# Side loads on a second queue, 64x64 taps in pairs, splits inside the norms, and routing over both token halves

## The chip, the cores and the metric

One Trainium2 chip, and one of its cores. The metric is the time of one execution of the kernel on the device, in microseconds; a kernel's time is the median over runs. A NeuronCore has separate engines with their own instruction streams: TensorE (PE), VectorE (DVE), ScalarE (ACT), GpSimd (POOL) and SyncE (SP). DMA transfers are issued from an engine's queue.

## The reference

Two blocks over 256 tokens of 1024 channels, in fp32. The part that matters here, with its parameters shortened:

```python
def conv_module(h, w_in, b_in, w_dw, b_dw, g_n, b_n, w_out, b_out):
    a, g = jnp.split(h @ w_in + b_in, 2, axis=-1)
    u = a * jax.nn.sigmoid(g)
    u = lax.conv_general_dilated(u, w_dw[:, None, :], window_strides=(1,), padding=[(CONV_K - 1, 0)],
        dimension_numbers=("NWC", "WIO", "NWC"), feature_group_count=u.shape[-1]) + b_dw   # 31 taps
    u = jax.nn.silu(layer_norm(u, g_n, b_n))
    return u @ w_out + b_out

def moe_swiglu(h, router_w, router_b, w13, w2):
    logits = (h @ router_w).astype(jnp.float32) + router_b.astype(jnp.float32)
    top_val, top_idx = lax.top_k(logits, TOP_K_EXPERTS)          # 2 of 8 experts
    top_w = jax.nn.softmax(top_val, axis=-1)
    gates = jnp.sum(jax.nn.one_hot(top_idx, N_EXPERTS) * top_w[..., None], axis=-2)
    for e in range(N_EXPERTS):
        y = y + gates[..., e:e + 1] * swiglu(h, w13[e], w2[e])
    return y

def first_block(x, c, ...):                                       # 256 tokens, 1024 channels, fp32
    c_act = jax.nn.silu(c)
    for l in range(2):
        sh1, sc1, g1, sh2, sc2, g2 = jnp.split(c_act @ ada_w[l] + ada_b[l], 6, axis=-1)
        h = x * (1.0 + sc1[:, None, :]) + sh1[:, None, :]
        out = conv_module(h, ...) if l == 0 else moba_attention(...) @ w_o[0]
        x = layer_norm(ALPHA * x + (1.0 + g1[:, None, :]) * out, ln_g[l, 0], ln_b[l, 0])
        h = x * (1.0 + sc2[:, None, :]) + sh2[:, None, :]
        f = swiglu(h, ffn_w13[0], ffn_w2[0]) if l == 0 else moe_swiglu(h, ...)
        x = layer_norm(ALPHA * x + (1.0 + g2[:, None, :]) * f, ln_g[l, 1], ln_b[l, 1])
    return x
# second_block: layer norm, band attention beside an rwkv7 scan, gates, layer norm,
# hier_moe (4 groups of 8 experts: the best group, 2 in it), layer norm, a gated projection, layer norm
```

## The kernel before

All weights are streamed. A list `units` holds them in the order of use, as pieces of 1 MB (128 partitions x 2048 fp32, two DMAs of 512 KB). SP issues their loads into the six slots of `ring_raw` as these come free. For fp32 accuracy, a product is three matmuls of rounded parts: ACT makes the high part of a unit (`split_hi`, into one of three slots of `ring_hi`, L442), DVE the low part (`split_lo`, `ring_lo`, L460), and PE's `columns` runs hi x hi, lo x hi and hi x lo (L2186 to L2188) per 128x128 block: 48 matmuls of 256 columns a unit. The activations have hi and lo parts too (`Hh`/`Hl`, `Gh`/`Gl`). The adaptive units ("ada": 24 for layer 0, 8 for kv, 24 for layer 1) aren't split: `adaptive` (L2223) multiplies an fp32 unit by the vector c on four column quarters of PE, and for each pair `turn_row` (L2236) turns ACT's copy of the row (`row_out`, L2507) into columns; DVE adds the bias (`biased`, L2867) to give `mods`.

The order is written out by hand, one list per engine, with semaphores between them. It goes:

1. start: ada 0 to 5 on PE, then transposes (L2243) of 40 short parameter rows (in `tA`) and of x (`tB`), ada 6 and 7, then ACT writes `Hh` (L2530) and DVE `Hl`. SP issues the ada loads, the row loads, x and the first router's loads (L1912) and then further units.
2. conv_in (8 units), then the depthwise convolution of 31 taps over 8 channel blocks. PE has three blocks and part of a fourth (`SHARED`, 17 taps): a tap is a matmul of a 128x128 diagonal with the shifted `uT` (L2315), all taps of a block summed in one bank. POOL writes the diagonals (L1820). DVE has the other blocks (`conv_dve`, L1806) and the rest of the shared one (L2904). `conv_order` puts five taps of PE behind each of the 16 ada units 8 to 23.
3. the conv norm: `ln_stats` on PE (mean L2264, variance L2270), `ln` on DVE (centre L2812, reciprocal L2818, scale L2823) with ACT squaring (L2476) between, `Gh`/`Gl`; then conv_out (4 units), ln0 of the same form, the FFN (11 pairs "ffn a"/"ffn b" and their down units), ln1, kv and q.
4. attention a1, interleaved with ada units of layer 1 by `between(i)`; the output product wo (4 units); ln2; and MoE m1: DVE ranks the logits (L1495 to L1507) for each half of the 128 tokens in turn, PE counts the chosen (L1214 to L1218), rows are gathered by matmul (L1237), and 56 groups of 6 units follow.
5. ln3, the second block with band attention and rwkv (L584, L610 are 64x64 matmuls of its chunked scan), MoE m2 (routing as in m1, 16 groups of 6 units), a gated projection and the output.

`ln` takes a function that it runs on DVE between the centre and the reciprocal, where DVE waits for PE's variance; m1's norm uses it, the conv norm and ln0 don't. `keep_busy` runs matmuls whose results nobody reads (L2252).

## Time and profile before

| | |
|---|---|
| median of 3 runs | 2388.09 us (2386.42 to 2390.18) |
| the profiled execution | 2391.7 us, its span 2389.9 us |
| busy share of the span | PE 95%, DVE 72%, ACT 58%, POOL 4% |
| mean granted clock of PE | 0.972 |
| chain that ended last | PE 88%, DVE 5%, ACT 3%, issue 2%, DMA 1%, SP's queue 1% |
| HBM | 257 GB/s over the span, 614 MB read |

The profile is of one execution, and its times are from the start of the span. "[2.32 <-ACT scr L2507]" means that the engine was idle for 2.32 us before the instruction, and what ended this. Short runs of one instruction are joined to a row with their count. A matmul of fp32 leaves two records, one of rounded operands one.

### The profile page before, as it was taken

Reading aid. Unit: us, or ns where it says so; the run is one execution under the profiler, and the core shown is the slowest. Engines: PE = TensorE matmul, PEld = TensorE weight load, DVE = VectorE, ACT = ScalarE, POOL = GpSimd, SP = SyncE. Lnnn points to the kernel's source line nnn. Section 1 sums busy time; section 2 is a strip of 40 time slices with the busy share of each in tenths; the row PEclk is TensorE's granted clock in tenths of the full one; section 3 lists DMA queues with packets and bytes.
Section 4 is the critical chain, followed back from the end, with each engine's and each line's share of the span. In section 5 each row is a group of like instructions: output and inputs, shape, how many; then the busy total and the mean of one; then the engine's idle time right before and its main releaser. Section 6 shows DMA issues by size and latency. Waiting matters only on the chain.

```text
span 2389.9 us, 36267 instructions
## 1 busy us (share of the span) xinstructions
PE 2274.6 (95%) x14695; PEld 1961.4 (82%) x14695; DVE 1730.1 (72%) x1723; ACT 1376.6 (58%) x1291; POOL 91.5 (4%) x140
## 2 busy tenths in 40 slices
PE   6997999998899999999999999999998897999998
PEld 4876999996788888888888888888997796888887
DVE  2885344636678888888888888884676467999954
ACT  3234333536567777777777777773465334777743
POOL 5600000001000000000000000000000000000000
PEclk9998999999899999999999999999999898999999
DMA  9665665359179999999999999995741231999930
GB/s 297 214 217 192 231 228 180 105 176 326 63 255 343 394 376 367 374 368 372 371 372 370 371 370 373 369 370 73 198 128 37 83 123 61 348 368 370 376 127 19
DMA packets 339267, 618.78 MB, mean 259 GB/s; under 512 B 24615, under 2 KB 165168, under 8 KB 339100
## 3 DMA queue, kind: packets, MB, share of 16 engines
q1 hardware_dynamic: 339100, 616.43, 73.9%
q8 instruction: 120, 1.97, 0.3%
q14 instruction: 47, 0.39, 0.0%
HBM read 614.26 MB, written 1.05 MB: 257 GB/s over the span
## 4 chain that ended last, share of the span: by engine, by line
PE 88%; DVE 5%; ACT 3%; issue 2%; DMA 1%; SPq 1%; DVEq 0%; ACTq 0%
PE bank L1264 11%; PE bank L1265 11%; PE bank L1266 11%; PE bank L2186 6%; PE bank L2187 6%; PE bank L2188 6%; PE bank L1296 6%; PE bank L1298 6%; PE bank L1294 6%; PE bank L2270 2%; PE bank L1237 1%; PE bank L2315 1%; PE bank L1274 1%; PE bank L1328 1%; PE bank L584 1%
## 5 line engine op out<-in xcount | busy, mean ns | idle before, releaser
L1379 DVE TENSOR_TENSOR ring_lo<-ring_raw,ring_hi 128x2048 fp32r<-128x2048 f32 x432 | 988.4, 2291 | 140.4 <-ACT ring_hi L1372 139.8
L1372 ACT ACTIVATE ring_hi<-ring_raw 128x2048 fp32r<-128x2048 f32 x432 | 828.0, 1920 | 297.3 <-PE bank L1266 177.2
L1264 PE MATMUL bank<-ring_hi,xg_hi 128*128 128x512 f32 x1152 | 458.2, 398 | 2.3 <-DVE xg_lo L1575 2.1
L1265 PE MATMUL bank<-ring_hi,xg_lo 128*128 128x512 f32 x1152 | 451.0, 391 | 0.0
L1266 PE MATMUL bank<-ring_lo,xg_hi 128*128 128x512 f32 x1152 | 450.9, 391 | 0.0
L2186 PE MATMUL bank<-Hh,ring_hi 128*128 128x256 f32 x1048 | 305.5, 291 | 31.0 <-DVE ring_lo L460 9.7
L460 DVE TENSOR_TENSOR ring_lo<-ring_raw,ring_hi 128x2048 fp32r<-128x2048 f32 (+1 forms) x96 | 217.9, 2283 | 138.7 <-ACT ring_hi L442 129.5
L2188 PE MATMUL bank<-Hh,ring_lo 128*128 128x256 f32 x1048 | 301.5, 288 | 0.0
L2187 PE MATMUL bank<-Hl,ring_hi 128*128 128x256 f32 x1016 | 292.8, 288 | 0.0
L1264 PEld LDWEIGHTS bank<-ring_hi,xg_hi 128*128 128x128 f32 x1152 | 217.5, 189 | 48.2 <-ACT xg_hi L1434 2.8
L1266 PEld LDWEIGHTS bank<-ring_lo,xg_hi 128*128 128x128 f32 x1152 | 217.1, 188 | 47.2
L1265 PEld LDWEIGHTS bank<-ring_hi,xg_lo 128*128 128x128 f32 x1152 | 217.6, 189 | 43.4
L2186 PEld LDWEIGHTS bank<-Hh,ring_hi 128*128 128x128 f32 x1048 | 206.3, 197 | 36.5 <-issue 24.7
L442 ACT ACTIVATE ring_hi<-ring_raw 128x2048 fp32r<-128x2048 f32 (+1 forms) x96 | 181.2, 1897 | 88.9 <-PE bank L2188 68.2
L1294 PE MATMUL bank<-ring_hi,mh 128*128 128x512 f32 x576 | 228.4, 396 | 0.0
L1296 PE MATMUL bank<-ring_hi,mh 128*128 128x512 f32 x576 | 228.2, 396 | 0.0
L1298 PE MATMUL bank<-ring_lo,mh 128*128 128x512 f32 x576 | 228.1, 396 | 0.0
L2188 PEld LDWEIGHTS bank<-Hh,ring_lo 128*128 128x128 f32 x1048 | 206.6, 197 | 0.0
L2187 PEld LDWEIGHTS bank<-Hl,ring_hi 128*128 128x128 f32 x1016 | 200.7, 198 | 0.1
L1298 PEld LDWEIGHTS bank<-ring_lo,mh 128*128 128x128 f32 x576 | 108.4, 188 | 26.2
L1296 PEld LDWEIGHTS bank<-ring_hi,mh 128*128 128x128 f32 x576 | 108.5, 188 | 25.8
L1294 PEld LDWEIGHTS bank<-ring_hi,mh 128*128 128x128 f32 x576 | 108.4, 188 | 25.7
(490 smaller groups left out, 2829.7 us busy)
## 6 DMA issues: line engine op xcount, KB each, us to landing
ring_raw<-in_moe_w SPq DMA_DIRECT2D x672, 512.0 KB, 5.3
ring_raw<-in_ada_w SPq DMA_DIRECT2D x96, 512.0 KB, 6.2
ring_raw<-in_ffn_w SPq DMA_DIRECT2D x66, 512.0 KB, 5.4
ring_raw<-in_exp_gate SPq DMA_DIRECT2D x64, 512.0 KB, 4.6
ring_raw<-in_exp_up SPq DMA_DIRECT2D x64, 512.0 KB, 4.7
ring_raw<-in_exp_down SPq DMA_DIRECT2D x64, 512.0 KB, 4.7
ring_raw<-in_w_in SPq DMA_DIRECT2D x42, 512.0 KB, 5.0
ring_raw<-in_conv_in_w SPq DMA_DIRECT2D x16, 512.0 KB, 8.1
```

Source lines behind the costliest of these rows:

```text
L460: nc.vector.tensor_tensor(ring_lo[:, i % SPLIT, 0:kt * c], ring_raw[:, n % RAW, 0:kt * c], ring_hi[:, i % SPLIT, 0:kt * c].bitcast(F32), A ...
L1264: mm(o, xg_hi[:, g, kk, :], wh(k), start=(kk == 0), stop=False)
L1265: mm(o, xg_lo[:, g, kk, :], wh(k), start=False, stop=False)
L1266: last = mm(o, xg_hi[:, g, kk, :], wl(k), start=False, stop=(kk == KT - 1))
L1294: mm(o, mh_hi[:, 2 * h + k, :], wh[:, k, ns], start=begin, stop=False, skip_group_check=True)
L1296: mm(o, mh_lo[:, 2 * h + k, :], wh[:, k, ns], start=False, stop=False, skip_group_check=True)
L1298: last = mm(o, mh_hi[:, 2 * h + k, :], wl[:, k, ns], start=False, stop=end, skip_group_check=True)
L1372: nc.scalar.activation(ring_hi[:, at % SPLIT, :], ring_raw[:, n % RAW, :], ACT.Copy)\
L1379: nc.vector.tensor_tensor(ring_lo[:, at % SPLIT, :], ring_raw[:, n % RAW, :], ring_hi[:, at % SPLIT, :].bitcast(F32), ALU.subtract).then_i ...
L2186: mm(o, wh[:, k, cs], Xh[:, k, :], start=(k == 0), stop=False)
L2187: mm(o, wh[:, k, cs], Xl[:, k, :], start=False, stop=False)
L2188: last = mm(o, wl[:, k, cs], Xh[:, k, :], start=False, stop=(k == kt - 1))
```

## The change

- **Loads.** x (now two DMAs) and the parameter rows are issued by ACT, right behind its first activation; SP keeps the units. The router's two loads stand ahead of conv_out 0's. PE runs ada 6 ahead of x's transposes.
- **Taps.** PE has four blocks whole or in part (the shared one, block 4, with 8 taps): 101 taps instead of 79. A diagonal is 128x64 (two 64x64 diagonals, one above the other). Taps go in pairs: of tap i the rows 0 to 63 and 64 to 127 are added to their own halves of the bank `dw`, of tap i+1 to the other halves of a bank `dx`. When a block is through, ACT copies `dx` to `scr`, and one matmul with a permutation (`perm`) adds it to `dw` with the halves swapped. Behind each ada unit stand three pairs, or four.
- **Norms.** In the conv norm and ln0, a `split_lo` of the next weight unit moves into the gap of `ln`, others move behind the halves that PE needs; `biased("turn kv")` comes behind the first pair of `affine_lo`. conv_out 0 waits for each k block by itself; `keep_busy` before it has 12 matmuls, not 20.
- **ffn and wo.** `biased("turn 1 1")` moves from the end of j = 3 to j = 4, behind `split_lo`. The splits of wo 0 move into the attention's last steps, `fold_in("m1")` behind them, and wo 0 waits for each head pair by itself.
- **Routing.** In m1 and m2 DVE's ranking takes both token halves in one instruction each; the counts take three matmuls, not five.

```diff
@@ -33,7 +33,7 @@
...
-PE_BLOCKS = 3
+PE_BLOCKS = 4
...
-            mm(b[:, 0:m.E], before[:, :], sel[:, 0, :], start=True, stop=True)
-            mm(b[:, m.E:2 * m.E], ones[:, :], sel[:, 0, :], start=True, stop=False)
-            mm(b[:, m.E:2 * m.E], before[:, :], sel[:, 1, :], start=False, stop=True)
-            for a in range(TT):
-                last = mm(b[:, 2 * m.E:3 * m.E], ones[:, :], sel[:, a, :], start=(a == 0), stop=(a == 1))
+            first_half = sel[:, 0:1, :].to_broadcast([P, TT, m.E])
+            mm(b[:, 0:2 * m.E], before[:, :], sel, start=True, stop=False, skip_group_check=True)
+            mm(b[:, m.E:3 * m.E], ones[:, :], first_half, start=False, stop=False, skip_group_check=True)
+            last = mm(b[:, 2 * m.E:3 * m.E], ones[:, :], sel[:, 1, :], start=False, stop=True, skip_group_check=True)
...
-            for a in range(TT):
-                rank(L[:, a, 0:E], 8, R, sel[:, a, 0:E])
-                ts(sel[:, a, 0:E], sel[:, a, 0:E], 1.5, None, ALU.is_lt).then_inc(dve.tick(), 1)
+            selE, shE = sel[:, :, 0:E], sh[:, :, 0:E]
+            by_group = lambda t: t[:, :, 0:E].rearrange("p a (g e) -> p (a g) e", e=8)
+            rank(by_group(L), 8, TT * R, by_group(sel))
...
+            T.mark(f"{nm} sel", *dve.last)
+            ts(shE, selE, -NEG, NEG, ALU.mult, ALU.add).then_inc(dve.tick(), 1)
+            dve.eng.wait_ge(*dve.own())
+            tt(shE, shE, L[:, :, 0:E], ALU.add).then_inc(dve.tick(), 1)
+            dve.eng.wait_ge(*dve.own())
+            nc.vector.tensor_reduce(rmax[:, :, 1:2], shE, AX, ALU.max, negate=True).then_inc(dve.tick(), 1)
...
-        SHARED, ON_PE = KT - PE_BLOCKS, 17
+        SHARED, ON_PE = KT - PE_BLOCKS, 8
         pe_taps = [(k, i) for k in pe_blocks for i in range(ON_PE if k == SHARED else TAPS)]
         last_tap = lambda k: ON_PE - 1 if k == SHARED else TAPS - 1
-        tiles = lambda t, n: [t[:, P * i:P * i + P] for i in range(n)]
-        diag = dict(zip(pe_taps, tiles(flat(GhF), 16) + tiles(flat(GlF), 16) + tiles(flat(convd), 16)
-                        + tiles(prF, 9) + tiles(prTF, 9) + tiles(flat(tB), 16) + tiles(flat(tD), 16)))
-        conv_order, taps_left = [], list(pe_taps)
+        tiles = lambda t, n: [t[:, 64 * i:64 * i + 64] for i in range(n)]
+        diag = dict(zip(pe_taps, tiles(flat(GhF), 32) + tiles(flat(GlF), 32) + tiles(flat(convd), 32) + tiles(prF, 18)))
+        tap_pairs = [(k, i) for k, i in pe_taps if i % 2 == 0]
+        swapped = scr[:, 1, :]
+        conv_order, taps_left, to_swap = [], list(tap_pairs), []
         for j in range(8, 24):
             conv_order.append(("ada", j))
-            for _ in range(5):
+            conv_order += [("swap", to_swap.pop(0)) for _ in range(len(to_swap))]
+            for _ in range(3 if j % 4 else 4):
                 if taps_left:
-                    conv_order.append(("tap", taps_left.pop(0)))
-        conv_order += [("tap", t) for t in taps_left]
+                    k, i = taps_left.pop(0)
+                    conv_order.append(("tap", (k, i)))
+                    if i + 2 > last_tap(k):
+                        to_swap.append(k)
+        assert not taps_left
+        conv_order += [("swap", k) for k in to_swap]
...
-            for n, (k, i) in enumerate(pe_taps):
-                if n == 66:
-                    pool.eng.wait_ge(*T.at("mm x 3"))
-                if n == 82:
-                    pool.eng.wait_ge(*T.at("Hl conv"))
-                nc.gpsimd.tensor_scalar(diag[k, i], ident[:, :], col("conv_dw_w", k, i), None, ALU.mult)\
+            for k, i in pe_taps:
+                nc.gpsimd.tensor_scalar(diag[k, i], m_one[:, :], col("conv_dw_w", k, i), None, ALU.mult)\
                     .then_inc(pool.tick(f"diag {k} {i}"), 1)
...
-                if what == "tap" and which[1] == last_tap(which[0]):
+                if what == "tap" and which[1] + 2 > last_tap(which[0]):
                     k = which[0]
                     act.eng.wait_ge(*T.at(f"mm dw {k}"))
+                    if k != SHARED:
+                        act.eng.wait_ge(*T.at(f"mm swap {k - 1}"))
+                    nc.scalar.activation(swapped, ps(f"dx {k}")[:, 0:S], ACT.Copy).then_inc(act.tick(f"ev dx {k}"), 1)
+                if what == "swap":
+                    k = which
+                    act.eng.wait_ge(*T.at(f"mm swap {k}"))
                     nc.scalar.activation(tA[:, k, :], ps(f"dw {k}")[:, 0:S], ACT.Identity, bias=col("conv_dw_b", k))\
...
@@ -1858,6 +1868,7 @@
...
+                if key == ("conv_out", 0):
+                    small_load("m1 router landed", rw[:, :, 0:8], A["router_w"][0].rearrange("(k p) n -> p k n", p=P))
+                    small_load("m1 router landed", rbias[:, 0:8], A["router_b"].to_broadcast([P, 8]))
...
+                            pe.eng.wait_ge(*T.at(f"hi {fresh} {k // 2 if fresh == 'convo' else k}"))
+                            pe.eng.wait_ge(*T.at(f"lo {fresh} {k if fresh == 'a1 o' else k // 2}"))
...
+            adaptive(0, 6, first)
...
-            for j in range(6, 8):
-                adaptive(0, j, first)
+            adaptive(0, 7, first)
...
+                if what == "swap":
+                    k = which
+                    pe.eng.wait_ge(*T.at(f"ev dx {k}"))
+                    mm(dw[:, 0:S], perm[:, :], swapped, start=False, stop=True, skip_group_check=True)\
+                        .then_inc(pe.tick(f"mm swap {k}"), 1)
+                    continue
...
-                    dw = take(pe, f"dw {k}", "C")
+                    dw, dx = take(pe, f"dw {k}", "C"), take(pe, f"dx {k}", "C")
                     pe.eng.wait_ge(*T.at(f"ev conv a {k // 2}"))
-                pe.eng.wait_ge(*T.at(f"diag {k} {i}"))
-                last = mm(dw[:, 0:S], diag[k, i], uT[:, k, i:i + S], start=(i == 0), stop=(i == last_tap(k)))
-                if i == last_tap(k):
-                    last.then_inc(pe.tick(f"mm dw {k}"), 1)
+                for tap in (i, i + 1):
+                    if tap > last_tap(k):
+                        continue
+                    pe.eng.wait_ge(*T.at(f"diag {k} {tap}"))
+                    for r in range(2):
+                        rows = slice(64 * r, 64 * r + 64)
+                        at = rows if tap == i else slice(64 - 64 * r, 128 - 64 * r)
+                        last = mm((dw if tap == i else dx)[at, 0:S], diag[k, tap][rows, :], uT[rows, k, tap:tap + S],
+                                  start=(i == 0), stop=(tap + 2 > last_tap(k)), skip_group_check=True)
+                        if tap + 1 > last_tap(k):
+                            last.then_inc(pe.tick(f"mm dw {k}"), 1)
...
-            keep_busy(20, "C")
-            pe.eng.wait_ge(*T.at("Gh conv"))
-            pe.eng.wait_ge(*T.at("Gl conv"))
+            keep_busy(12, "C")
             for j in range(4):
-                columns(("conv_out", j), f"out0 {j}", Gh, Gl)
+                columns(("conv_out", j), f"out0 {j}", Gh, Gl, None if j else "convo")
...
-            pe.eng.wait_ge(*T.at("Hh wo"))
-            pe.eng.wait_ge(*T.at("Hl wo"))
             for j in range(4):
-                columns(("wo", j), f"wo {j}", Hh, Hl)
+                columns(("wo", j), f"wo {j}", Hh, Hl, None if j else "a1 o")
...
+            x_in = tB[:, :, :].rearrange("p (a k) t -> p a (k t)", a=TT)
+            for a in range(TT):
+                small_load("x landed", x_in[:, a, :], A["x"][0, a * P:(a + 1) * P, :])
+            rows = tA[:, 0:4, :].rearrange("p k t -> p (k t)")
+            act.eng.wait_ge(*T.at("rows cleared"))
...
+            for name, src, n, width in sources:
+                r = ROW[name]
+                small_load("rows landed", rows[r:r + n, 0:width], src)
...
+                if i == 16:
+                    split_hi(act, at_unit[("wo", 0)])
...
                 for j in range(4):
+                    if j == 1 and behind_first:
+                        behind_first()
...
-            conv_dve(dve, range(2, KT - PE_BLOCKS), done)
-            dve.eng.wait_ge(*T.at(f"ev dw {SHARED}"))
-            for i in range(ON_PE, TAPS):
-                stt(tA[:, SHARED, :], uT[:, SHARED, i:i + S], col("conv_dw_w", SHARED, i), tA[:, SHARED, :],
-                    ALU.mult, ALU.add).then_inc(dve.tick(f"z conv {SHARED}"), 1)
-                dve.eng.wait_ge(*dve.own())
+            for i in range(ON_PE):
+                done[SHARED, i] = T.at(f"ev dw {SHARED}")
+            conv_dve(dve, range(2, KT - PE_BLOCKS + 1), done)
+            def in_conv_norm():
+                split_lo(dve, at_unit[("conv_out", 0)])
+                biased("turn rest", [(0, v) for v in range(2, 6)])
+            ln("conv", None, in_conv_norm)
+            halves_lo("convo", Gl, tD, Gh)
             split_lo(dve, at_unit[("conv_out", 1)])
-            biased("turn rest", [(0, v) for v in range(2, 6)])
-            ln("conv")
-            halves_lo("convo", Gl, tD, Gh)
             T.mark("Gl conv", *dve.last)
             dve.eng.wait_ge(*T.at("mods 0 2"))
             tt(gb[:, :], cols[:, :, ROW["conv_out_b"]], mods[:, VEC(0, 2), :], ALU.mult).then_inc(dve.tick("gb"), 1)
             fold_in("ffnin")
             residual("ln0", "out0", "conv_out")
+            ln("ln0", None, lambda: split_lo(dve, at_unit[("ffn a", 0)]))
+            affine_lo("ffnin", tD, Hl, Hh, lambda: biased("turn kv", [(2, 0), (2, 1)]))
+            T.mark("Hl ffn", *dve.last)
...
-            biased("turn kv", [(2, 0), (2, 1)])
...
+                    if j == 4:
+                        biased("turn 1 1", [(1, 1)])
...
-                if j == 3:
-                    biased("turn 1 1", [(1, 1)])
...
-                    fold_in("m1")
+                    split_lo(dve, at_unit[("wo", 0)])
...
+            fold_in("m1")
```

What stands in three places, as each engine's list of instructions gives it. On PE, at the start of the convolution's taps (`uT` the shifted input, `GhF`/`GlF` the diagonals), before:

```order
L2223 MATMUL bank<-ring_raw,scr 32x256 x8
L2315 MATMUL bank<-uT,GhF 128x256 x5
L2223 MATMUL bank<-ring_raw,scr 32x256 x8
L2315 MATMUL bank<-uT,GhF 128x256 x5
L2223 MATMUL bank<-ring_raw,scr 32x256 x8
```

and in the changed kernel:

```order
L2204 MATMUL bank<-ring_raw,scr 32x256 x8
L2308 MATMUL bank<-uT,GhF 64x256 x16
L2204 MATMUL bank<-ring_raw,scr 32x256 x8
L2294 MATMUL bank<-scr,perm 128x256
L2308 MATMUL bank<-uT,GhF 64x256 x12
L2204 MATMUL bank<-ring_raw,scr 32x256 x8
```

Five whole matmuls behind an ada unit became 16 or 12 of a quarter, and the swap of block 4 comes behind the next ada unit. On DVE, ln0 and what leads to the first FFN unit (L2812 and L2818 are the norm, L2774 and L2778 `affine_lo`, L2867 `biased`), before:

```order
L460 TENSOR_TENSOR ring_lo<-ring_raw,ring_hi 128x2048 x2
L2812 TENSOR_TENSOR tA<-tA,bank 128x512 x4
L2818 RECIPROCAL stat<-stat 128x256
L2823 TENSOR_TENSOR tA<-tA,stat 128x512 x4
L2774 TENSOR_SCALAR tD<-tA,fold 128x256 x2
L2778 TENSOR_TENSOR Hl<-tD,Hh 128x512
...
L2835 TENSOR_SCALAR xT<-tA,cols 128x256 x8
L2867 TENSOR_TENSOR mods<-bank,cols 128x8 x2
L460 TENSOR_TENSOR ring_lo<-ring_raw,ring_hi 128x2048 x2
```

and in the changed kernel, with other line numbers:

```order
L2843 TENSOR_TENSOR tA<-tA,bank 128x512 x4
L461 TENSOR_TENSOR ring_lo<-ring_raw,ring_hi 128x2048
L2849 RECIPROCAL stat<-stat 128x256
L2854 TENSOR_TENSOR tA<-tA,stat 128x512 x4
L2805 TENSOR_SCALAR tD<-tA,fold 128x256 x2
L2809 TENSOR_TENSOR Hl<-tD,Hh 128x512
L2898 TENSOR_TENSOR mods<-bank,cols 128x8 x2
...
L461 TENSOR_TENSOR ring_lo<-ring_raw,ring_hi 128x2048
L2866 TENSOR_SCALAR xT<-tA,cols 128x256 x8
```

One split stands behind the centre, the other behind `affine_lo`, and the `mods` behind its first pair.

## Rows read from the trace of the kernel before

**Rows 1.** Busy time by stretch: PE, PEld, DVE, ACT, POOL, granted clock, DMA share, GB/s.

```profile
60.00:97.00 37.00, 37.00 (x310) 36.90 (x308) 26.96 (x41) 10.05 (x11) 37.00 (x45) 1.00 0.56 181
97.00:157.00 60.00, 60.00 (x477) 42.21 (x476) 56.93 (x141) 6.87 (x13) 1.68 (x3) 1.00 0.84 273
...
700.00:1000.00 300.00, 299.81 (x1342) 245.22 (x1342) 264.72 (x146) 222.69 (x147) 1.59 (x2) 1.00 1.01 371
```

**Rows 2.** PE's waits in the first 60 us: in total, times, longest.

```profile
PE bank L2223 <- DMA ring_raw<-in_ada_w: 11.0, 6, 4.1
```

**Rows 3.** Timeline of SP's queue: start, us, what it issues.

```profile
24.67 3.13 SPq L1912 DMA_DIRECT2D rbias<-in_router_b  x1
```

**Rows 4.** Timeline of PE, ada 2 and ada 5.

```profile
14.52 1.94 PE L2223 MATMUL bank<-ring_raw,scr 128*32 128x256 f32 x16 [1.08 <-DMA ring_raw<-in_ada_w]
...
23.51 1.93 PE L2223 MATMUL bank<-ring_raw,scr 128*32 128x256 f32 x16 [0.37 <-DMA ring_raw<-in_ada_w]
```

**Rows 5.** The chain that ended last: start, us, what.

```profile
42.21 1.92 ACT ring_hi L442
...
98.11 2.36 PE bank L2315 x10
100.46 1.00 PE bank L2223 x16
...
108.18 0.98 PE bank L2236 x8
...
183.12 0.21 PE bank L2188
```

**Rows 6.** Timeline of PE in the rwkv scan, 64x64 matmuls.

```profile
1826.98 0.69 PE L610 MATMUL bank<-tB,tC 64*64 64x64 f32 x32 [0.44 <-ACT HhF L2701]
1827.50 0.65 PE L610 MATMUL bank<-tC,tB 64*64 64x64 f32 x32
...
1843.36 0.66 PE L584 MATMUL bank<-tD,relb 64*64 64x64 f32 x16
1843.83 0.66 PE L584 MATMUL bank<-pr,prT 64*64 64x64 f32 x16
```

**Rows 7.** Timeline of DVE: taps' end, conv norm, ln0, modulations of kv.

```profile
148.25 7.25 DVE L2904 SCALAR_TENSOR_TENSOR tA<-uT,cols,tA 128x256 f32<-128x256 f32 x14
...
161.62 2.29 DVE L460 TENSOR_TENSOR ring_lo<-ring_raw,ring_hi 128x2048 fp32r<-128x2048 f32 x1 [0.17 <-ACT ring_hi L442]
...
211.06 4.49 DVE L460 TENSOR_TENSOR ring_lo<-ring_raw,ring_hi 128x2048 fp32r<-128x2048 f32 x2 [1.10 <-issue]
...
228.65 0.73 DVE L2774 TENSOR_SCALAR tD<-tA,fold 128x256 f32<-128x256 f32 x2
```

**Rows 8.** Timeline of PE: conv norm, conv_out 0, ln0, ffn a 0.

```profile
165.62 5.38 PE L2270 MATMUL bank<-tC,means 128*128 128x256 f32 x16 [3.28 <-ACT tC L2476]
...
181.57 0.36 PE L2186 MATMUL bank<-Gh,ring_hi 128*128 128x256 f32 x1 [2.32 <-ACT scr L2507]
...
216.95 5.38 PE L2270 MATMUL bank<-tC,means 128*128 128x256 f32 x16 [4.05 <-ACT tC L2476]
...
236.10 0.58 PE L2186 MATMUL bank<-Hh,ring_hi 128*128 128x256 f32 x1 [8.30 <-DVE mods L2867]
```

**Rows 9.** Timeline of DVE, the FFN's pair 3.

```profile
314.78 0.17 DVE L2867 TENSOR_TENSOR mods<-bank,cols 128x8 f32<-128x8 f32 x1 [7.42 <-PE bank L2236]
```

**Rows 10.** Timeline of PE at wo 0.

```profile
588.35 0.55 PE L2186 MATMUL bank<-Hh,ring_hi 128*128 128x256 f32 x1 [4.75 <-DVE ring_lo L460]
```

**Rows 11.** Timeline of DVE, m1's routing.

```profile
633.26 0.23 DVE L1495 TENSOR_TENSOR tC<-pr 128x64 f32<-128x64 f32 x1
...
634.63 0.23 DVE L1495 TENSOR_TENSOR tC<-pr 128x64 f32<-128x64 f32 x1
```

**Rows 12.** Timeline of DVE, m2's routing.

```profile
1978.17 0.42 DVE L1495 TENSOR_TENSOR tC<-pr 128x256 f32<-128x256 f32 x1
...
1981.90 0.42 DVE L1495 TENSOR_TENSOR tC<-pr 128x256 f32<-128x256 f32 x1
```

More of the change, by code:

```diff
@@ L1901, in softmax_rest @@
                                 ALU.subtract).then_inc(dve.tick(f"ev {name} o {k}"), 1)
+                    T.mark(f"lo {name} o {k}", *dve.last)
         block = ctx.enter_context(nc.Block())
@@ L2059, in _ @@
             eng.memset(tA[:, 0:4, :], 0.0).then_inc(pool.tick("rows cleared"), 1)
+            for k in range(2):
+                b0 = slice(64 * k, 64 * k + 64)
+                pool.eng.wait_ge(*pool.own())
+                eng.tensor_copy(m_one[b0, :], ident[b0, b0]).then_inc(pool.tick(), 1)
+                pool.eng.wait_ge(*pool.own())
+                eng.tensor_copy(perm[:, b0], ident[:, 64 - 64 * k:128 - 64 * k]).then_inc(pool.tick(), 1)
             eng.memset(means[:, :], 1.0 / D).then_inc(pool.tick("means"), 1)
@@ L2110, in stack @@
                 pool.eng.wait_ge(*pool.own())
-            for k in range(2):
-                b0 = slice(64 * k, 64 * k + 64)
-                pool.eng.wait_ge(*pool.own())
-                eng.tensor_copy(m_one[b0, :], ident[b0, b0]).then_inc(pool.tick(), 1)
-            pool.eng.wait_ge(*pool.own())
             for m, sign, op, n in ((m_su, 1, ALU.is_gt, 64), (m_sl16, -1, ALU.is_gt, 16), (m_iu, 1, ALU.is_ge, 64)):
@@ L2513, in _, with small_load @@
             T.mark("ccol", *act.last)
+            def small_load(label, dst, src):
+                eng.dma_start(dst, src).then_inc(T.sem(label), 16)
+                T.count[label] = T.count.get(label, 0) + 16
+                T.mark(label, label, T.count[label])
+            x_in = tB[:, :, :].rearrange("p (a k) t -> p a (k t)", a=TT)
[3 more added lines that the diff above has]
+            act.eng.wait_ge(*T.at("rows cleared"))
+            sources = [
+                ("conv_dw_w", A["conv_dw_w"][0], TAPS, D), ("conv_dw_b", A["conv_dw_b"], 1, D),
+                ("conv_norm_g", A["conv_norm_g"], 1, D), ("conv_norm_b", A["conv_norm_b"], 1, D),
+                ("conv_out_b", A["conv_out_b"], 1, D),
+                ("conv_in_b", A["conv_in_b"].rearrange("a (r d) -> (a r) d", d=D), 2, D),
+                ("ada_b", A["ada_b"].rearrange("a (r d) -> (a r) d", d=D), 12, D),
+                ("kv_ada_b", A["kv_ada_b"].rearrange("(r d) -> r d", d=D), 2, D),
+                ("ln_g", A["ln_g"].rearrange("a b d -> (a b) d"), 4, D),
+                ("ln_b", A["ln_b"].rearrange("a b d -> (a b) d"), 4, D),
+                ("ln_in_g_2", A["ln_in_g_2"].rearrange("(r d) -> r d", r=1), 1, D),
+                ("ln_in_b_2", A["ln_in_b_2"].rearrange("(r d) -> r d", r=1), 1, D),
+                ("ln_g_2", A["ln_g_2"][0], 3, D), ("ln_b_2", A["ln_b_2"][0], 3, D),
+                ("tok_mix_2", A["tok_mix_2"][:, 0:D], 1, D),
+            ]
+            for name, src, n, width in sources:
+                r = ROW[name]
+                small_load("rows landed", rows[r:r + n, 0:width], src)
+            r = ROW["tok_mix_2"] + 1
+            rest = A["tok_mix_2"].shape[1] - D
+            small_load("rows landed", rows[r:r + 1, 0:rest], A["tok_mix_2"][:, D:D + rest])
+            small_load("rows landed", rows[r + 1:r + 2, 0:P], A["tok_mix_2"][:, D + rest - P:D + rest])
+            for name in ("decay_base_2", "aaa_base_2", "k_k_2", "k_a_2", "gn_g_2", "gn_b_2"):
+                r = ROW[name]
+                small_load("rows landed", rows[r:r + 1, 0:512], A[name])
+            r = ROW["r_k_2"]
+            small_load("rows landed", rows[r:r + 1, 0:512], A["r_k_2"].rearrange("a h d -> a (h d)"))
             for p in range(3):
@@ L2915, in _ @@
             residual("ln0", "out0", "conv_out")
+            ln("ln0", None, lambda: split_lo(dve, at_unit[("ffn a", 0)]))
+            affine_lo("ffnin", tD, Hl, Hh, lambda: biased("turn kv", [(2, 0), (2, 1)]))
+            T.mark("Hl ffn", *dve.last)
             split_lo(dve, at_unit[("ffn b", 0)])
-            ln("ln0")
-            affine_lo("ffnin", tD, Hl, Hh)
-            T.mark("Hl ffn", *dve.last)
             affine("ln_g", "ln_b", 0)
-            biased("turn kv", [(2, 0), (2, 1)])
             dve.stage = "ffn"
```

84 lines of the change are left out of this document (23 added, 61 removed).

## The prediction

> **What bounds the kernel now.** I read the page first (PE busy 95% of the span, 88% of the chain that ended last), then the windows, then PE's waits and the timelines around each wait. From 700 to 1000 us PE is busy for 299.81 of 300 us in MoE m1 [rows 1], and so it goes on through the groups of both MoE stages. There the change edits nothing, and no wait on a DMA follows that could swallow a gain made earlier, so each microsecond that PE is released earlier ahead of it should arrive at the end. All that the change can win lies in the places where PE idles or does dear work: the start (it waits 11.0 us for ada units [rows 2]), the taps from 97 to 154 us, two norms, one FFN pair, wo and two routings.
>
> **The start: 5.7 us (3 to 7).** Ada 2 starts at 14.52 and ada 5 at 23.51, each after a wait for its data [rows 4]: 3.0 us for a unit of 1 MB, or some 350 GB/s. The first conv_in unit is used from 42.21 [rows 5]. In the 18.7 us between 23.51 and 42.21 land three units, x (1 MB) and 0.3 MB of rows by their shapes: 4.3 x 3.0 = 12.9 us. The other 5.8 us the DMA engines don't work, because SP issues 27 small loads one behind the other, with the router's bias at 3.13 us [rows 3], before it comes to ada 6. From ACT's queue they are issued beside SP's. Everything must still pass, so the ada units are spread out by x, but the bubble goes. ACT has nothing to do until the row of ada 0 and 1, and its 29 issues (0.25 to 0.3 us each, an estimate from SP's short ones) end about when this row is due; ACT's later rows have slack, since PE waits for data there. The Trainium skill says, in "DMA: Bandwidth & Descriptors", section "Issuing engines are not separate DMA queues", that queues share the 16 DMA engines and a second issuer only saves issue time; the sum here is of that saved time alone, and by the page's "usually small" it would be near 0, which makes the rival below. The router's loads, now before conv_out 0's, are hidden by a ring of six units.
>
> **The taps: 6.4 us (0 to 8).** From 97.11 to the end of ada 23 at 153.83 the chain is 16 ada units of 1.00, six turns of 0.98, and 75 taps, five in 2.36 us, so 0.472 each [rows 5]: 57.3 by the sum, 56.7 as measured. Afterwards the same stretch has 16.0 + 5.9 of these, 49 pairs and three swaps with a stall each: bank group C has two banks, so the next block's pair waits for ACT's eviction behind the swap, about 0.8 us (0.57 for a copy like ACT's others and the hops). The price of a pair is what the trace of before doesn't show. It is four matmuls of 256 columns, one on each 64x64 quadrant. From below: ada's matmuls run four at a time on column quarters, 8 in 1.00 us, so 0.50 for four. The scan's L610 has 32 records, 16 matmuls of 64 columns on four quadrants, in 0.52 us [rows 6]; four times the columns for four matmuls is again 0.52. There the two row halves write banks of their own. In a pair both row halves write `dw` at once (its diagonal quadrants), and both write `dx`. L584 does just this with two quadrants: 8 matmuls of 64 columns in 0.47 us (1843.36 to 1843.83), 59 ns each. A matmul of 256 columns alone takes 472 ns, so one of 64 some 118: they do overlap two by two although they share a bank. I take 0.50. From above, if they didn't overlap across a shared bank, a pair would be 0.94. With 0.50: 16.0 + 5.9 + 24.5 + 1.5 + 2.4 = 50.3 us. The Trainium skill, "TensorEngine Tiling (Array Packing)", section "Gotcha 1: PSUM Pressure", says that different row tiles cannot access the same PSUM bank simultaneously; L584's row speaks against a cost of this, and with the rule the term would turn from a gain into a loss (second rival).
>
> Who else must keep up: DVE has 56.93 us of 60 busy in 97 to 157, 141 instructions, 0.40 each [rows 1], and at the end 14 dependent taps in 7.25 us [rows 7]. It has 22 taps fewer (147 for 169), 9 us, against the 6 to 7 us by which PE ends earlier, and the serial tail is gone; it stays just ahead. POOL makes 101 diagonals of half the width instead of 79; at 37.00/45 = 0.82 us for a full one [rows 1] all would be there within 83 us of some 30, and half the width should be cheaper; block 4's and 5's are needed first. DMA carries 0.84 of its time at 273 GB/s [rows 1]; 16 units in 50.3 us are 3.1 each, just above 3.0, with six in the ring. So no new bound, but little margin: a pair below 0.45 would win nothing more.
>
> **The conv norm: 3.7 us (3 to 4.4); conv_out 0: 2.9 us (1.8 to 4.4).** Before the centre DVE runs two splits, the second 161.62 to 163.9 [rows 7], for the landing of conv_out 1. PE waits 3.28 for ACT's squares and then runs L2270 in 5.38 us, at half clock for the most part, against 3.6 us at full [rows 8]. With the centre straight behind the mean the idle time goes to about 2 and L2270 gets cheaper. The split in the gap costs 2.29, less than the 4.9 us that DVE waits there. Then PE waits 2.32 for ACT and the halves, until 181.57, and pays 0.21 us [rows 5] instead of 37.00/310 = 0.12 [rows 1] for its first matmuls, 15 of them. Starting k by k, as `Gh` and `Gl` come 1.6 us apart, gives the start some 4 us earlier and the end about 2.9, since the last quarter is as late as before.
>
> **ln0: 4.8 us (3.4 to 5.2).** Two splits, 4.49 us from 211.06, stand before the centre, for which the mean was ready at about 211.3; PE waits 4.05 [rows 7, 8]. Both go from there: 4.2 us, and 0.6 of clock. One of 2.29 in the gap is hidden as before.
>
> **ffn a 0: 6.2 us (5.2 to 7.4).** PE waits 8.30 us until 236.10, for `mods` in a bank [rows 8], although the first pair of `affine_lo` is through before 228.65 [rows 7], plus 0.7 for its low part. With `biased` there PE can start at about 229.9. The three other pairs come every 1.45 us, and a group of 12 matmuls for two k at 0.12 to 0.21 takes 1.4 to 2.5, so it isn't starved again.
>
> **ffn pair 3: 2.5 us (1 to 3).** DVE idles 7.42 us until 314.78 for a turn of PE [rows 9] with three splits queued behind it, the first of which PE then waits for 2.6. One `split_lo` now goes ahead.
>
> **wo 0: 5.5 us (4 to 6).** PE waits 4.75 for the split, until 588.35 [rows 10], then 20 matmuls run at 0.21: 1.8 of clock. Splitting inside the attention hides it, behind DVE's idle time there; of the 6.5 I take 5.5, as the last head pair's halves still come late. `fold_in("m1")` (four instructions of 0.17) is needed only at ln2.
>
> **Routing: 1.8 us in m1, 3.2 in m2 (together 3 to 6).** The ranks of a half start 1.37 us apart in m1 and 3.73 in m2 [rows 11, 12]. One chain goes each time. The wider instructions of the other cost more: m2's 256 elements take 0.42, and 512 elements 0.7 by DVE's other rows, five times 0.27 = 1.35. That leaves 2.4 and 1.2; the second chain of shifts isn't awaited, and two counting matmuls with their latency give 0.6 to 0.8 each.
>
> **Sum.** 5.7 + 6.4 + 3.7 + 2.9 + 4.8 + 6.2 + 2.5 + 5.5 + 1.8 + 3.2 = 42.7 us. The profiled execution took 2391.7, 3.6 above the median; so 2349.0 in its terms, and 2345.4 as a median: 2345. With the lower ends of all terms it is 26 us, with the upper ones 52; as they don't all fall together, 2336 to 2356 is this case's own range.
>
> **Rivals.**
> - **The start wins nothing, and the clock isn't given back.** For: x and the rows now compete with ada 0 to 5, ACT's issues could hold up its own rows, and PE, with work spread thinner, has a slower clock when the columns begin. Against: the 5.8 us of no transfer. Without 5.7, and without some 5 us of the clock shares in the norms, ffn a 0 and wo: 2356.
> - **Row halves don't overlap on a shared bank.** A pair 0.94: 49 x 0.44 = 21.6 us more in the stretch, and 1.3 for the three pairs behind it, so 22.9: 2368. Against: L584 [rows 6].
> - **Slower: quadrants run one at a time**, because start flags, rows of weights and accumulation in fp32 force each of 202 to its full 0.472. A pair is 1.9; 52 x 1.4 = 73 us more: 2418. It decides from a pair of 0.50 + 42.7/52 = 1.3 us on. Against: both kinds of row in [rows 6].
>
> **How the numbers follow.** The forecast's case 0.72, the start and the clock 0.12, the shared bank 0.12, all serial 0.04. The range is 2334 to 2365: it takes in the first rival, leaves out the shared bank's and the serial one, and the rest of the forecast's tail. Within 0.2% is 4.8 us, about what a measurement here can tell from no change; only a pair price near 1.3 would land there, 0.01. Faster 0.95, slower 0.04.
>
> **What would show it.** Columns of conv_in start near 44 instead of 49.7. From the first ada behind conv_in to the end of ada 23: 50 us, with 16 records of L2308's first row in 2.0 us; 3.8 would be the shared bank. PE's waits on `tC` fall to about 2 and 0 to 1; the one on `mods` at the first FFN unit to about 0; the 4.75 at wo to under 1. PE idles about 3 us less at m2's count. If DVE's taps or DMA end last in the convolution, that term was wrong; if a new wait on `ring_lo` appears behind ffn a 0, a moved split was too late.

## The result and the profile after

The changed kernel takes 2347.13 us (median of 4 runs, 2345.28 to 2354.05), the kernel before beside it 2389.14 (2386.42 to 2390.2): a ratio of 0.9824, 95% interval 0.981 to 0.9839, so 42 us less, where 2345 was forecast. The profiled execution of after took 2345.28 with a span of 2343.6, that of before 2391.7 with 2389.9: 46.3 us between the two spans, which the readings below account for.

The windows of after: us, then PE, PEld, DVE, ACT and POOL busy, granted clock, DMA share, GB/s. The stretches of [rows 1] are among them.

```profile
0.00:60.00 60.00, 36.39 (x297) 26.50 (x298) 15.91 (x27) 19.54 (x25) 30.33 (x62) 0.97 0.96 306
60.00:97.00 37.00, 37.00 (x322) 36.22 (x325) 25.45 (x41) 10.81 (x12) 37.00 (x67) 1.00 0.51 167
97.00:157.00 60.00, 57.49 (x756) 35.79 (x749) 50.92 (x124) 15.14 (x23) 1.34 (x3) 1.00 0.87 282
...
700.00:1000.00 300.00, 300.00 (x1342) 245.56 (x1341) 265.70 (x146) 222.21 (x148) 0.00 (x0) 1.00 1.03 377
```

m1 is as full as before: 1342 matmuls in 300 us in both. What was gained ahead of it came through. PE's waits in the first 60 us answer to [rows 2]:

```profile
PE bank L2204 <- DMA ring_raw<-in_ada_w: 14.1, 3, 8.5
PE bank L2204 <- POOL lower L2063: 3.9, 1, 3.9
PE bank L2167 <- DVE Hl L2916: 2.8, 2, 2.4
```

PE waits longer for ada units than before, not shorter: 14.1 against 11.0 by these rows, and the 3.9 is the wait for ada 0 too, which before is in the 11.0 with 4.1; so 18.0 against 11.0. PE's timeline, and SP's queue in the fence behind it, tell when, as [rows 3, 4] do for before:

```profile
13.80 1.94 PE L2204 MATMUL bank<-ring_raw,scr 128*32 128x256 f32 x16 [5.11 <-DMA ring_raw<-in_ada_w]
24.26 1.93 PE L2204 MATMUL bank<-ring_raw,scr 128*32 128x256 f32 x16 [8.53 <-DMA ring_raw<-in_ada_w]
26.63 1.93 PE L2204 MATMUL bank<-ring_raw,scr 128*32 128x256 f32 x16 [0.44 <-DMA ring_raw<-in_ada_w]
```

```profile
9.51 7.55 SPq L1933 DMA_DIRECT2D ring_raw<-in_ada_w  x1
```

One issue of SP, an ordinary half unit, takes 7.55 us, and ada 2, which started at 14.52 before, starts at 24.26. The bubble between ada 5 and 6 is gone and another stands ahead of ada 2. In transfer time the two are nearly equal. Before, DMA moved 122 and 212 GB/s in 20 to 25 and 25 to 30 us; in the changed kernel it moved 228, 209 and 285 GB/s in 15 to 20, 20 to 25 and 25 to 30. Measured against some 350 GB/s, that is 5.2 us lost before and 4.7 after (an estimate). The chain of after, which answers to [rows 5]:

```profile
41.10 1.92 ACT ring_hi L443
...
95.75 1.00 PE bank L2204 x16
96.75 1.89 PE bank L2308 x32
98.64 1.04 PE bank L2204 x16
99.71 0.60 ACT scr L2497
100.31 0.48 ACT tA L1841
100.84 1.53 PE bank L2308 x24
...
103.36 1.46 PE bank L2308 x24
...
143.92 1.05 PE bank L2204 x16
```

The splitting of the first conv_in unit starts at 41.10 instead of 42.21, the first ada of the convolution at 95.75 instead of 97.11: 1.4 us. Sixteen quarter matmuls (32 records) take 1.89 us and twelve 1.46, so a pair (four of them) takes 0.47 to 0.49. A swap with its waits costs 1.1 to 1.2 us, here from 99.68 to 100.84. Ada 23 ends at about 144.95; the stretch takes 49.2 us, before 56.7.

The timelines of PE and DVE after it, for [rows 7, 8, 10, 12]:

```profile
154.54 3.69 PE L2251 MATMUL bank<-tC,means 128*128 128x256 f32 x16 [0.30 <-ACT tC L2466]
...
167.21 0.36 PE L2167 MATMUL bank<-Gh,ring_hi 128*128 128x256 f32 x1 [0.70 <-DVE Gl L2796]
...
207.36 0.44 PE L2167 MATMUL bank<-Hh,ring_hi 128*128 128x256 f32 x1 [1.14 <-DVE mods L2898]
...
552.93 0.36 PE L2167 MATMUL bank<-Hh,ring_hi 128*128 128x256 f32 x1 [0.81 <-issue]
```

```profile
158.78 1.75 DVE L2849 RECIPROCAL stat<-stat 128x256 f32<-128x256 f32 x1 [0.86 <-ACT stat L2473]
...
201.30 1.75 DVE L2849 RECIPROCAL stat<-stat 128x256 f32<-128x256 f32 x1 [1.38 <-ACT stat L2473]
...
1934.25 0.23 DVE L1481 TENSOR_TENSOR pr<-bank,rbias 128x64 f32<-128x64 f32 x1 [2.24 <-PE bank L1201]
1934.39 0.15 DVE L1483 TENSOR_TENSOR pr<-bank,rbias 128x8 f32<-128x8 f32 x1
1934.58 0.69 DVE L1494 TENSOR_TENSOR tC<-pr 128x512 f32<-128x512 f32 x1
```

The waits of 3.28, 4.05, 8.30 and 4.75 us are 0.30, 0.5, 1.14 and 0.81. The norm's second product takes 3.69 instead of 5.38: the granted clock is 1.00 in 154.5 to 158.2, where it was 0.68 in 165.6 to 171 before. Ahead of it PE stood idle for 0.30 us, before for 3.28. Reading the same places in both traces (before's reciprocals stand at 171.54 and 222.88) gives the gain piece by piece:

| piece, from and to | before | after | gain | forecast |
|---|---|---|---|---|
| span's start to the first ada of the convolution | 97.11 | 95.75 | 1.4 | 5.7 |
| to the end of ada 23 | 56.7 | 49.2 | 7.5 | 6.4 |
| to the conv norm's reciprocal | 17.7 | 13.8 | 3.9 | 3.7 |
| to the end of conv_out 0 | 17.5 | 13.9 | 3.6 | 2.9 |
| to ln0's reciprocal | 33.8 | 28.6 | 5.2 | 4.8 |
| to the end of ffn a 0 | 21.5 | 14.4 | 7.1 | 6.2 |
| to the end of the attention's last product | 339.2 | 336.4 | 2.8 | 2.5 |
| to the end of wo 0 | 12.7 | 6.9 | 5.8 | 5.5 |
| to m1's first up product | 64.3 | 61.9 | 2.4 | 1.8 |
| to the end of the span | 1729.3 | 1722.7 | 6.6 | 3.2 |

### The profile page after: what moved, and what is told of

It reads as the page before. It is cut to its first block, busy times and chain, and to the rows that moved or that the text cites. A ratio compares the mean times of both kernels' runs of the same rounds, so it can differ in the third digit from the quotient of the medians.

```text
span 2343.6 us, 36726 instructions
## 1 busy us (share of the span) xinstructions
PE 2244.6 (96%) x14925; PEld 1929.1 (82%) x14925; DVE 1715.0 (73%) x1672; ACT 1377.8 (59%) x1296; POOL 88.3 (4%) x164
## 4 chain that ended last, share of the span: by engine, by line
PE 89%; DVE 4%; ACT 3%; DMA 2%; issue 1%; SPq 1%; DVEq 0%; ACTq 0%
PE bank L1264 11%; PE bank L1265 11%; PE bank L1266 11%; PE bank L2167 6%; PE bank L2168 6%; PE bank L2169 6%; PE bank L1296 6%; PE bank L1298 6%; PE bank L1294 6%; PE bank L1237 1%; PE bank L2251 1%; PE bank L2204 1%; PE bank L1274 1%; PE bank L1328 1%; PE bank L585 1%
## 5 line engine op out<-in xcount | busy, mean ns | idle before, releaser
L2167 PE MATMUL bank<-Hh,ring_hi 128*128 128x256 f32 x1048 | 303.3, 289 | 17.7 <-DVE Hl L2809 9.3
```

The costliest lines, as they stand in the source:

```text
L2167: mm(o, wh[:, k, cs], Xh[:, k, :], start=(k == 0), stop=False)
```

## Experiments

Twelve further kernels ran, one of them the changed kernel again, all beside runs of the kernel before. They start from the changed kernel; their edits are shown shortened. Single executions of one kernel differ by up to 12 us (the changed kernel's: 2345.1 to 2356.7), so that where a few us matter, the places in the traces are compared and not the totals alone. Five of the times are of one execution and are named so.

### Each part turned back

**The start.** x, rows and router loads on SP's queue as before, ada 6 behind x's transposes.

```diff
-            for a in range(TT):
-                small_load("x landed", x_in[:, a, :], ...)      # in ACT's program
-            ... 24 row loads
+            ... the same on SP, behind load(0) to load(5)
-            adaptive(0, 6, first)                               # ahead of x's transposes
```

> The changed kernel with its loads as before: x, the rows and the router's loads on SP's queue, ada 6 behind x's transposes. The prediction's term for this part is 5.7 us: 2347 + 5.7 = 2353. The trace of the changed kernel says otherwise: the first ada of the convolution starts at 95.75 instead of 97.11, so 1.4 us: 2348.5, and that first ada at 97.1 again.

Measured: 2346.0 us (0.9825 of before, 0.9806 to 0.9844), no slower than the changed kernel. The first ada of the convolution starts at 96.73. This part of the change brings nothing that these runs can tell from zero.

**The taps.**

```diff
-PE_BLOCKS = 4
+PE_BLOCKS = 3
-        SHARED, ON_PE = KT - PE_BLOCKS, 8
+        SHARED, ON_PE = KT - PE_BLOCKS, 17
```

and with it whole diagonals, no `dx` and no swap, and the 14 serial taps of DVE.

> The changed kernel with the convolution's taps as before (79 whole diagonals on PE, 169 taps on DVE). By the prediction's term 6.4 us slower: 2353.5; by the trace of the changed kernel, where the stretch from the first ada to the end of ada 23 takes 49.2 us instead of 56.7, 7.5: 2354.5. Rival: DVE, which gets its 14 serial taps back, now ends last ahead of the norm, because the start and the rest are earlier: then 9 or more, 2356.

Measured: 2354.05 (0.9851, 0.9835 to 0.9868), about 7 us slower than the changed kernel. From the first ada (97.98) to the end of ada 23 (154.70) it takes 56.7 us again. The rows from there to the mean's product follow on each other without a wait, so DVE does not end last:

```profile
153.70 1.00 PE bank L2192 x16
154.70 0.98 PE bank L2205 x8
155.69 1.84 PE bank L2284 x8
157.52 0.79 PE bank L2205 x8
158.31 3.58 PE bank L2233 x16
```

**The splits and biases.**

```diff
-            ln("conv", None, in_conv_norm)
-            halves_lo("convo", Gl, tD, Gh)
-            split_lo(dve, at_unit[("conv_out", 1)])
+            split_lo(dve, at_unit[("conv_out", 1)])
+            biased("turn rest", [(0, v) for v in range(2, 6)])
+            ln("conv")
+            halves_lo("convo", Gl, tD, Gh)
```

and the same way back in ln0, ffn a 0, ffn pair 3 and wo 0. With it come the waits of conv_out 0 and wo 0 for all of their halves at once, and `keep_busy(20, "C")`.

> The changed kernel with all moves of splits and of biased turned back (conv norm, conv_out 0, ln0, ffn a 0, ffn pair 3, wo 0). By the prediction's terms 3.7 + 2.9 + 4.8 + 6.2 + 2.5 + 5.5 = 25.6 us slower: 2372.7. By the trace of the changed kernel 3.9 + 3.6 + 5.2 for the first three and about 15.8 for the rest, 28.5: 2375.6. Rival: part of it is clock that was given back by chance, then nearer 22: 2369.

Measured: 2378.55 (0.9956, 0.9943 to 0.9969), 31 us slower than the changed kernel, by far the largest part. PE's waits from 150 to 260 us, all of them:

```profile
PE bank L2165 <- DVE mods L2896: 8.3, 1, 8.3
PE bank L2249 <- ACT tC L2468: 7.8, 2, 4.1
PE bank L2165 <- ACT scr L2499: 2.3, 1, 2.3
PE bank L2292 <- ACT scr L1837: 0.5, 1, 0.5
```

The old waits stand there with their old lengths (8.30; 3.28 and 4.05 became 7.8 in two; 2.32), although the start and the taps before them are the new ones. Further on PE waits for `ring_lo` for 2.59 us in FFN pair 3 and for 4.75 at wo 0, as before the change (2.59 and 4.75); the changed kernel has neither wait. So they don't depend on the other parts of the change.

**The routing.**

```diff
-            rank(by_group(L), 8, TT * R, by_group(sel))
+            for a in range(TT):
+                rank(L[:, a, 0:E], 8, R, sel[:, a, 0:E])
```

> The changed kernel with the routing of m1 and m2 for each token half and five counting matmuls. By the prediction's terms 1.8 + 3.2 = 5.0 us slower: 2352. Rival: the chain of ACT's logits copy and the exponentials covers part, then 3: 2350.

Measured: 2355.87 (0.9851, 0.9834 to 0.9868). That is 9 us more than the changed kernel, but the trace doesn't give 9 to the routing. In m2 it takes 15.0 us from the first logits (1943.69) to the gather (1958.69), in the changed kernel 11.8 (1934.25 to 1946.02): 3.2. In m1 the same way takes 8.1 us; in the kernels with the new routing it is 6.6 to 7.5, so 0.6 to 1.5.

The profiled execution is 12.7 us longer than that of the changed kernel. 2.4 of it stands ahead of the convolution: the first ada is at 98.1, with the start of the changed kernel. Another 6.3 stands at ln3, where PE waits 6.13 us for DVE instead of 2.63 and then runs the mean's product at a granted clock of 0.56 instead of 1.00. The same place in this kernel, in the one with ACT held back (below), whose edit is 1.6 ms earlier, and in the changed kernel:

```profile
1614.04 6.53 PE L2246 MATMUL bank<-tA,means 128*128 128x256 f32 x16 [6.13 <-DVE tA L3012]
```

```profile
1612.79 6.61 PE L2245 MATMUL bank<-tA,means 128*128 128x256 f32 x16 [6.14 <-DVE tA L3012]
```

```profile
1608.15 3.69 PE L2245 MATMUL bank<-tA,means 128*128 128x256 f32 x16 [2.63 <-DVE tA L3011]
```

Of the fourteen traces three have the long wait (6.13 or 6.14), the others 1.1 to 2.6. So it comes and goes between executions and is not the routing's. DVE stands there behind the branch that closes m1 (`value_load` and `If`); why it sometimes stands 3.5 us longer wasn't found.

### What quarters cost when row halves share a bank

Both taps of a pair go to the same two diagonal quadrants and the same bank; no `dx`, no swap.

```diff
-                        at = rows if tap == i else slice(64 - 64 * r, 128 - 64 * r)
-                        last = mm((dw if tap == i else dx)[at, 0:S], ...
+                        last = mm(dw[rows, 0:S], ...
```

> The changed kernel with both taps of a pair on the same two diagonal quadrants, all into one bank, and no second bank and no swap. If quadrants of different row halves overlap although they write one bank, as L584's row says, a pair's four matmuls take two times 0.47, 0.94 us, and three pairs 2.8 instead of 1.46. If a bank that two row halves share makes them wait, 1.9 a pair, three pairs 5.7. The stretch from the first ada to the end of ada 23 would be 16.0 + 5.9 + 49 x 0.94 = 68 us in the first case, 115 in the second.

Measured: one execution, 2365.07. The chain's rows of the first ada units:

```profile
97.85 1.00 PE bank L2198 x16
98.85 3.60 PE bank L2297 x32
102.45 1.00 PE bank L2198 x16
103.45 2.74 PE bank L2297 x24
```

Three pairs take 2.74 us, 0.91 a pair, where four matmuls of 0.472 one behind the other would be 1.89 (an estimate): two quadrants overlap although their row halves write one bank. Crossing the quadrants halves the pair to 0.49. From the first ada to the end of ada 23 it is 65.6 us without crossing and 49.2 with it, the swaps included.

### Why the start brings nothing

The Trainium skill ("DMA: Bandwidth & Descriptors", section "Issuing engines are not separate DMA queues") says that a second issuer saves only issue time. Here not even that was saved, so five kernels look at what SP's issues do.

**ACT held back** until ada 1 is done: `act.eng.wait_ge(T.sem("unit_done"), 2)` ahead of its loads.

> The changed kernel, but ACT waits with its 29 issues for the end of ada 1. Theory: what swallowed the start's 5.7 us is that SP's issues stand still while ACT's queue is full (one took 7.5 us in the changed kernel), so that ada 2 comes at 24 us instead of 14.5. Held back, ada 2 and 3 land at 14.5 and 17.5; whether the stall only moves behind them is the question. If it doesn't, the first ada of the convolution starts near 92; if it does, near 96 as in the changed kernel. Rival, that the time is the volume over the rate, whatever the order: 96 in any case.

Measured: 2351.03 (0.9832, 0.9816 to 0.9849). Ada 2 and 3 are on time (13.81, 16.82), but then one issue of SP takes 8.11 us, and the first ada of the convolution starts at 99.1. The stall moved with ACT's loads, which are now issued from 12.81 to 21.3 us, as SP's queue shows:

```profile
23.03 8.11 SPq L1933 DMA_DIRECT2D ring_raw<-in_ada_w  x1
```

**x on SP's queue, the rows on ACT's.**

> The changed kernel with the rows alone on ACT's queue and x on SP's behind ada 5. If it is the 27 small loads that stop SP's issues, an issue of several us stays in SP's queue and ada 2 still lands after 20. If it is x's megabyte, ada 2 lands at 14.5 to 16 and no issue of SP takes over 2 us; the first ada of the convolution then starts at 92 to 95.

Measured: an issue of SP of 9.44 us at 7.26, ada 2 at 21.83, the first ada of the convolution at 96.3; one execution, 2345.97.

**The rows on SP's queue behind ada 5, x on ACT's.**

> The changed kernel with x alone on ACT's queue and the rows on SP's behind ada 5. If the small loads on a second queue stop SP's issues, none takes over 2 us here and ada 2 comes about 3 us later than before, at 17.5, by x's volume alone; if x does it, ada 2 lands after 20 as in the changed kernel.

Measured: the longest issue 4.03 us, ada 2 at 16.36, ada 5 at 25.66, but ada 6 at 35.87 behind the rows; the first ada of the convolution at 96.4; one execution, 2346.09. The longest issue was to be under 2 us, so that number was missed; before it is 3.2 with everything on SP's queue. The timeline:

```profile
16.36 1.93 PE L2233 MATMUL bank<-ring_raw,scr 128*32 128x256 f32 x16 [1.08 <-DMA ring_raw<-in_ada_w]
```

So the long stall comes with the rows on the second queue, not with x there.

**Five rows behind each of the first five units on SP's queue, x on ACT's.**

```diff
+            for n in range(RAW):
+                load(n)
+                for dst, src in smalls[:5]:
+                    small_load("rows landed", dst, src)
+                del smalls[:5]
```

> The changed kernel with the 24 row loads on SP's queue again, but five behind each of the first five ada units, and x alone on ACT's queue. Theory: small loads pass slowly (the DMA engines carried 100 to 140 GB/s while they had them alone), and nothing is lost where big transfers of the same queue stand before and behind them. Then the ada units come some 2 to 3 us later each, the bubble of 20 to 30 us is gone, and the first ada of the convolution starts at about 92: 5 us less than with the rows behind ada 5, 2342. Rival: a queue with small loads in it is as slow wherever they stand, then 96 and no gain on the changed kernel.

Measured: 2349.51 (0.9825, 0.9811 to 0.9838), the same as the changed kernel beside it (2349.42). The first ada of the convolution starts at 97.8, so the theory (92) was wrong and the rival (96) near. One row load's issue takes 6.12 us:

```profile
5.23 6.12 SPq L1924 DMA_DIRECT2D tA<-in_conv_in_b  x1
```

and the windows from 10 to 15 and 15 to 20 us have 211 and 293 GB/s, where the kernel with the rows behind ada 5 has 357 and 348.

**Ten row loads instead of 24.**

> The changed kernel with 10 row loads on ACT's queue instead of 24; the parameters of the second block (its norms, mixing and decay rows) are left out, so what depends on them is not the reference's. If the number of small loads sets how long SP's issue stands still, the stall of 7.5 to 10 us falls to 3 to 4; if it is any small load on a second queue or x's megabyte, it stays over 7.

Measured: SP's issue still takes 9.07 us, ada 2 starts at 23.25, the first ada of the convolution at 96.5. So the number of small loads doesn't set the length of the stall. (With the second block's parameters missing its time as a whole, 3834 us in one execution, says nothing.)

### The same kernel again, and the clock

> The changed kernel itself once more, to be compared on the same chip with the version above: 2347 by its first runs, the first ada of the convolution at 95.7 to 99.6 as in the runs that share its start.

Measured: 2349.42 (0.9825, 0.9805 to 0.9844), the first ada of the convolution at 95.8. From the reciprocal of the second norm behind m1 to that of the norm ahead of m2's routing it takes 4.3 us longer than in the first trace of the same kernel (300.4 against 296.1), and the granted clock there, in 1820 to 1870 us, is 0.80 where it was 0.86.

**Without the 12 matmuls ahead of conv_out 0** (`keep_busy(12, "C")` left out).

> The changed kernel without the 12 matmuls that keep PE busy ahead of conv_out 0. PE is then idle for 2.9 us where it waits for the halves. If what conv_out 0 gains beside the wait is the clock (15 matmuls of it at 0.21 instead of 0.12 us before the change), the slow pitch comes back and the unit ends about 1.4 us later than in the changed kernel; if the clock doesn't follow such a gap, nothing changes.

Measured: one execution, 2354.1, within the changed kernel's spread, with the first ada of the convolution at 99.2. PE's timeline:

```profile
168.08 0.55 PE L2167 MATMUL bank<-Gh,ring_hi 128*128 128x256 f32 x1 [2.16 <-DVE Gl L2795]
168.43 0.41 PE L2168 MATMUL bank<-Gl,ring_hi 128*128 128x256 f32 x1
168.64 0.41 PE L2169 MATMUL bank<-Gh,ring_lo 128*128 128x256 f32 x1
...
172.95 0.36 PE L2167 MATMUL bank<-Gh,ring_hi 128*128 128x256 f32 x1 [0.66 <-DVE Gl L2795]
```

After the gap the slow pitch is there (0.21 us; the granted clock is 0.52 in 168 to 171.5, almost all of it at 1.2 GHz, the lower of TensorE's two levels). But from the reciprocal (162.87) to the turn behind the unit (176.61) it takes 13.74 us, in the changed kernel 13.75 (158.78 to 172.53). I had expected 1.4 more if the slow pitch came back. Both kernels wait for the last quarter of `Gl`, 10.08 us behind the reciprocal in both (here 172.95), and the slow matmuls lie in front of that wait.

## Why the forecast came out, and where it was wrong

**The total is right partly by luck.** The forecast's sum was 42.7 and 42.0 was measured, but one term of 5.7 is missing, and the others brought more: by the two traces 41.5 for 37.0. The rest of the traces' 46.3 is 1.4 at the start and 3.4 that belong to no edit. (The range that the prediction gives for its sum is misadded: the lower ends make 24.4 and the upper ones 51.4, not 26 and 52.)

**The start is the step that failed:** "Everything must still pass, so the ada units are spread out by x, but the bubble goes." Turning it back costs nothing (2346.0), and the first columns of conv_in start at 47.28 instead of 48.19, where the prediction's sign was near 44. In the seven profiled executions of kernels with exactly this start the first ada of the convolution stands at 95.75, 95.8, 97.8, 98.0, 98.1, 99.2 and 99.6, 97.7 on the mean; with everything on SP's queue at 97.1 and 96.7. The estimate of the bubble was right (5.8 forecast, 5.2 by the transfer rates). But it doesn't go when the issues go to another queue: with the rows on ACT's queue an issue of SP takes 7.5 to 10.2 us in ten executions of ten, and with them on SP's queue behind ada 5 none takes over 4.1 in three of three. ACT's loads were 26, not 29 as in the prediction, and they were all issued by 11.7 us, so ACT's own issue time is not what stood in the way. The first rival had this in its first half, with a chance of 0.12. Its second half, that the clock isn't given back, did not come, so the time was not its 2356.

**The taps:** right in mechanism, 7.5 instead of 6.4. The pair was 0.47 to 0.49, for 0.50, and a swap 1.1 to 1.2, for 1.3. DVE and DMA kept up: DVE's last tap ends near 143.9 and the mean's product starts at 149.2, and PE never waits for an ada unit there. The second rival is refuted twice, by the pair and by the uncrossed kernel: quadrants of different row halves overlap on one bank, as was worked out from L584 in [rows 6]. The rule of the Trainium skill ("TensorEngine Tiling (Array Packing)", section "Gotcha 1: PSUM Pressure"), that different row tiles cannot access the same bank simultaneously, shows no cost in time in any trace here.

**The splits:** right in mechanism at all six places: 3.9 for 3.7, 3.6 for 2.9, 5.2 for 4.8, 7.1 for 6.2, 2.8 for 2.5 (in a piece of 336 us), 5.8 for 5.5. Together 28.4 by the two traces, against 25.6 forecast; turning all back costs 31. No new wait on `ring_lo` came behind ffn a 0. In the conv norm two misses cancel: PE's idle time fell to 0.30 where about 2 was forecast, but the swap of the last block and its wait, which no term of the sum has, put the mean's product 4.2 us behind ada 23 instead of 3.5. The largest miss is ffn a 0, 0.9 too small: I had added 0.7 us for the first low part to 228.65, but that is where the second pair begins [rows 7], and the low part is through then. PE starts ffn a 0 6.06 us behind the reciprocal (201.30 to 207.36), before it was 13.22. For conv_out 0, "the last quarter is as late as before" holds, and the kernel without `keep_busy` shows that the clock was no part of the gain.

**The routing:** m2 15.0 to 11.8 us, 3.2 as forecast. In m1 the way from the logits to the gather went from 9.1 to 7.2 us, and turned back it is 8.1, so 1.9 by the two traces and 0.6 to 1.5 by the kernel turned back, for 1.8; the 2.4 of the table is in a piece that also holds ln2. The rest of the last line of the table, some 3.4 us between m1 and the end, belongs to no edit. 2.7 of it stands between the second norm behind m1 and the norm ahead of m2's routing, where the granted clock differs: 0.81 in 1859 to 1909 before, 0.86 in the same piece of work (1820 to 1870) after. The changed kernel's second trace has 0.80 there and is 4.3 us longer than its first in that piece. So it is the luck of one execution, and it accounts for most of why the two spans differ by 46.3 and the medians by 42.0.

The slower rival needed a pair of 1.3 us; it is 0.49.

## What to carry to other kernels

Price each wait where it stands and ask what PE has queued behind it: moves of one or two instructions at six places, each worth 3 to 7 us, brought 28 to 31 of 42 us, and each price could be read from the trace of before to within 1 us. A transfer bubble is not priced by its length alone: before a move to another queue is charged with the whole of it, one kernel with that move alone should show whether the other queue keeps running. And where a later wait sets the end of a piece of work, the slow clock ahead of it costs nothing.
